# Joints between layer stages of a decoder kernel: tiles in pairs, norm factors in ScalarE's copies, one strip's split in halves

## What is computed

```
def _rmsnorm(x, g):
    xf = x.astype(jnp.float32)
    y = xf * lax.rsqrt(jnp.mean(xf * xf, axis=-1, keepdims=True) + NORM_EPS)
    return (y * g.astype(jnp.float32)).astype(x.dtype)
...
        xp = xp + _rmsnorm(mp, gn[1])
        xs = xs + _rmsnorm(ms, gn[1])
        xp = xp + _rmsnorm(_mlp(_rmsnorm(xp, gn[2]), w_ff1[layer], w_ff2[layer]), gn[3])
        xs = xs + _rmsnorm(_mlp(_rmsnorm(xs, gn[2]), w_ff1[layer], w_ff2[layer]), gn[3])
```

## Time and profile before

| | |
|---|---|
| time, median of 3 runs (lowest, highest) | 1041.13 us (1038.32, 1041.52) |
| the profiled execution's own time | 1040.35 us |
| its span | 1038.5 us |
| PE busy (matmul) | 979.0 us, 94% |
| VectorE busy | 604.4 us, 58% |
| ScalarE busy | 434.8 us, 42% |
| DMA, mean | 199 GB/s |
| mean granted TensorE clock | 0.981 of full |

### The profile page before, as it was taken

One profiled execution on the slowest core, in us unless ns is written; L12 is line 12 of the kernel. 1 busy time (PEld: TensorE's weight loads), 2 busy tenths in 40 slices (PEclk: granted clock), 3 DMA queues, 4 the chain that ended last, 5 costly groups with the idle time before them and its releaser, 6 DMA issues. The chain is left out here.

```text
span 1038.5 us, 17317 instructions
## 1 busy us (share of the span) xinstructions
PE 979.0 (94%) x7348; PEld 893.3 (86%) x7348; DVE 604.4 (58%) x767; ACT 434.8 (42%) x549; POOL 35.4 (3%) x72
## 2 busy tenths in 40 slices
PE   6999999998979999999789999999999799999994
PEld 5888998654979999999787878778799799999993
DVE  6756644547487554334775767586573775543443
ACT  5222233567455444333532443526343554543330
POOL 0310000000000000000001000000100000000000
PEclk9999999999989999999899999999999899999997
DMA  9887859636525444544544948685755244444411
GB/s 357 307 287 260 275 166 359 225 109 227 200 90 184 164 168 172 172 170 165 196 168 152 328 170 308 238 286 187 277 208 186 95 167 167 174 171 171 163 40 45
DMA packets 50444, 206.60 MB, mean 199 GB/s; under 512 B 3536, under 2 KB 3920, under 8 KB 34768
## 3 DMA queue, kind: packets, MB, share of 16 engines
q1 hardware_dynamic: 44640, 181.40, 50.0%
q0 software_dynamic: 5744, 24.33, 6.0%
HBM read 181.39 MB, written 24.33 MB: 198 GB/s over the span
## 5 line engine op out<-in xcount | busy, mean ns | idle before, releaser
L563 PE MATMUL banks<-hH,wH 128*128 128x288 f32 x1248 | 378.7, 303 | 29.8 <-DVE hL L1522 26.4
L1153 ACT ACTIVATE wH<-raw 128x2048 fp32r<-128x2048 f32 x116 | 222.2, 1916 | 376.8 <-PE banks L565 374.5
L1513 DVE TENSOR_TENSOR wL<-raw,wH 128x2048 fp32r<-128x2048 f32 x116 | 265.8, 2291 | 195.9 <-ACT wH L1153 195.7
L564 PE MATMUL banks<-hL,wH 128*128 128x288 f32 x1248 | 371.4, 298 | 0.0
L565 PE MATMUL banks<-hH,wL 128*128 128x288 f32 x1248 | 371.4, 298 | 0.0
L563 PEld LDWEIGHTS banks<-hH,wH 128*128 128x128 f32 x1248 | 239.5, 192 | 47.4 <-issue 40.1
L564 PEld LDWEIGHTS banks<-hL,wH 128*128 128x128 f32 x1248 | 238.3, 191 | 0.4
L565 PEld LDWEIGHTS banks<-hH,wL 128*128 128x128 f32 x1248 | 237.9, 191 | 0.0
L564 PE MATMUL banks<-aL,wH 128*128 128x288 f32 x512 | 151.0, 295 | 0.0
L565 PE MATMUL banks<-aH,wL 128*128 128x288 f32 x512 | 150.9, 295 | 0.0
L563 PE MATMUL banks<-aH,wH 128*128 128x288 f32 x512 | 150.2, 293 | 0.0
(11 more groups left out here) (265 smaller groups left out, 1012.9 us busy)
## 6 DMA issues: line engine op xcount, KB each, us to landing
raw<-wst SPq DMA_DIRECT2D x120, 1024.0 KB, 4.9
cache_sb<-kcache SPq DMA_DIRECT2D x14, 1024.0 KB, 6.1
sslot<-state SPq DMA_DIRECT2D x11, 1024.0 KB, 7.3
sstate_out<-sslot POOLq DMA_DIRECT2D x11, 1024.0 KB, 8.5
raw<-vcache SPq DMA_DIRECT2D x6, 1024.0 KB, 9.6
w_area<-vcache SPq DMA_DIRECT2D x6, 1024.0 KB, 13.0
raw<-state SPq DMA_DIRECT2D x5, 1024.0 KB, 8.2
sstate_out<-raw POOLq DMA_DIRECT2D x5, 1024.0 KB, 5.5
```

What stands on the lines that cost most here:

```text
L563: nc.tensor.matmul(out[:, m, :], wH[:, u % 2, c], hi[:, k, :], start=first, stop=False)
L564: nc.tensor.matmul(out[:, m, :], wH[:, u % 2, c], lo[:, k, :], start=False, stop=False)
L1153: nc.scalar.activation(wH[:, at % SPL, :], raw[:, raw_slot(at), :], ACT.Copy).then_inc(h_round, 1)
L1513: nc.vector.tensor_tensor(wL[:, at % SPL, :], raw[:, raw_slot(at), :], wH[:, at % SPL, :].bitcast(F32), ALU.subtract).then_inc(l_split, 1)
```

## The change

- **Gain.** `copy_y` multiplies by the post-norm gain while ScalarE copies y out of PSUM, one tile at a time. `residual` then needs only `y * rs_post` and the addition, both in place without `tmp`.
- **Groups.** `residual` runs over `X_GROUPS`: tiles 0 and 1 alone, then three pairs; at the end of the kernel over four pairs. The hL of a group stands behind the *next* group's multiplication. ScalarE's `pre_norm` follows the same groups, with one square for a pair.
- **Second strip.** Its split leaves the middle of the tiles and stands behind them, in two halves (`low_split`, `l_split`); PE's wL matmuls of that strip run tile by tile and wait for the halves in turn.
- **Third strip.** Its first half's split stands ahead of the three sums of squares; PE takes `mean_square` behind the fifth tile, not the second.
- **Retention.** `qpad` is cleared after p = 2, and strip 5 is split after p = 3.
- **x_out** is issued and waited for by SP, not POOL.

Nothing is put into PE's pause at a joint.

```diff
+X_GROUPS = ((0, 1), (1, 1), (2, 2), (4, 2), (6, 2))
+X_LAST = ((0, 2), (2, 2), (4, 2), (6, 2))
...
             strips(S_RETOUT + N_RETOUT, N_STRIPS)
+            for k, n in X_LAST:
+                sp.wait_ge(x_done, 3 * KT + k + n)
+                sp.dma_start(x_out[:, k:k + n, :], x[:, k:k + n, :]).then_inc(fin, 16)
+            sp.wait_ge(fin, 16 * len(X_LAST))
...
-            for k in range(0, KT, 2):
-                pool.wait_ge(x_done, 3 * KT + k + 2)
-                pool.dma_start(x_out[:, k:k + 2, :], x[:, k:k + 2, :]).then_inc(fin, 16)
-            pool.wait_ge(fin, 16 * KT // 2)
...
-                pe.wait_ge(l_split, s + 2)
-                for m in range(2):
-                    for k in range(KT):
+                pe.wait_ge(low_split, b)
+                for k in range(KT):
+                    if k == KT // 2:
+                        pe.wait_ge(l_split, s + 2)
+                    for m in range(2):
...
-                    if k == 1:
+                    if k == KT // 2:
                         mean_square(mean_d, sumsq[:, :], x_sum, 3 * b)
...
-                for k in range(KT):
-                    act.wait_ge(x_done, KT * (b - 1) + k + 1)
-                    round_x(k, layer, norm)
-                    nc.scalar.activation(y[:, k, :], x[:, k, :], ACT.Square).then_inc(xsq2, 1)
+                for k, n in X_GROUPS:
+                    act.wait_ge(x_done, KT * (b - 1) + k + n)
+                    for i in range(k, k + n):
+                        round_x(i, layer, norm)
+                    nc.scalar.activation(y[:, k:k + n, :], x[:, k:k + n, :], ACT.Square).then_inc(xsq2, n)
...
+            def copy_y(e, k, of):
+
+                return nc.scalar.activation(y[:, k, :], of, ACT.Copy, scale=gain(*POST_NORM[e], k))
+
...
-                nc.scalar.activation(y[:, 2 * j:2 * j + 2, :], out, ACT.Copy).then_inc(y_copied, 1)
+                copy_y(e, 2 * j, out[:, 0, :])
+                copy_y(e, 2 * j + 1, out[:, 1, :]).then_inc(y_copied, 1)
...
-                    dve.wait_ge(xsq2, KT * b)
-                    nc.vector.tensor_tensor(y[:, 0:4, :], y[:, 0:4, :], y[:, 4:8, :], ALU.add).then_inc(x_sum, 1)
                     dve.wait_ge(half_round, b + 1)
                     c = slice(0, HALF_STRIP)
                     nc.vector.tensor_tensor(wL[:, s % 2, c], raw[:, raw_slot(s + 2), c], wH[:, s % 2, c].bitcast(F32),
                                             ALU.subtract).then_inc(half_split, 1)
+                    dve.wait_ge(xsq2, KT * b)
+                    nc.vector.tensor_tensor(y[:, 0:4, :], y[:, 0:4, :], y[:, 4:8, :], ALU.add).then_inc(x_sum, 1)
...
-                for k in range(KT + 2):
-                    if k < KT:
-                        if k >= 2:
-                            dve.wait_ge(x_done, KT * e + k - 1)
-                        nc.vector.scalar_tensor_tensor(out=tmp[:, k % 2, :], in0=y[:, k, :], scalar=gain(layer, norm, k),
-                                                       in1=rs_post[:, :], op0=ALU.mult, op1=ALU.mult).then_inc(t_done, 1)
-                    if 1 <= k <= KT:
-                        dve.wait_ge(t_done, KT * e + k)
-                        nc.vector.tensor_tensor(x[:, k - 1, :], x[:, k - 1, :], tmp[:, (k - 1) % 2, :],
-                                                ALU.add).then_inc(x_done, 1)
-                    if k >= 2 and b is not None:
-                        split_x(b, k - 2, nlayer, nnorm)
-                    if k == 4 and s is not None:
-                        split_strip(s + SPL, s + SPL)
+                groups = X_LAST if b is None else X_GROUPS
+                behind = ()
+                for k, n in groups:
+                    c = slice(k, k + n)
+                    rs = rs_post[:, :].unsqueeze(1).broadcast_to([P, n, T])
+                    nc.vector.tensor_tensor(y[:, c, :], y[:, c, :], rs, ALU.mult).then_inc(t_done, n)
+                    for i in behind:
+                        split_x(b, i, nlayer, nnorm)
+                    dve.wait_ge(t_done, KT * e + k + n)
+                    nc.vector.tensor_tensor(x[:, c, :], x[:, c, :], y[:, c, :], ALU.add).then_inc(x_done, n)
+                    behind = range(k, k + n) if b is not None else ()
+                for i in behind:
+                    split_x(b, i, nlayer, nnorm)
+                if b is None:
+                    return
+
+                at = (s + SPL) % SPL
+                dve.wait_ge(h_round, s + SPL + 1)
+                for c, done in ((slice(0, HALF_STRIP), low_split), (slice(HALF_STRIP, KT * SC), l_split)):
+                    nc.vector.tensor_tensor(wL[:, at, c], raw[:, raw_slot(s + SPL), c], wH[:, at, c].bitcast(F32),
+                                            ALU.subtract).then_inc(done, 1)
...
-                if p == 3:
-                    nc.vector.memset(qpad[:, :, :], 0.0).then_inc(r_dec, 1)
...
                 if p == 2:
-                    split_strip(s + 3, s + 3)
+                    nc.vector.memset(qpad[:, :, :], 0.0).then_inc(r_dec, 1)
+                if p == 3:
+                    split_strip(s + 2, s + 2)
```

16 lines of the change are left out of this document (9 added, 7 removed).

## The result

The changed kernel takes 1033.28 us (median of 4 runs, 1032.43 to 1033.70), beside 1040.73 us for the kernel before in the same series (4 runs, 1038.32 to 1041.52): a ratio of 0.9929, 95% interval 0.9915 to 0.9944. It is faster by about 7.4 us. The forecast was 1035.1 us in a range of 1032.3 to 1038.3.

A forecast was written before the change was run, and what follows sets the result against it. PE, busy 94% of the span, was taken as the bound, so only its waits and half clock mattered. The terms summed to -5.63 us, giving 1034.7 or 1035.5 by starting point; forecast 1035.1 us, range 1032.3 to 1038.3.

The forecast's parts named there:

- Part 1: Start of the three joints: the first hL comes earlier and PE moves with it, -0.57 us each.
- Part 2: Third strip in joints 1 and 3: sums ahead of the second half's split make PE wait, +0.43 us each.
- Part 3: Head 0 of retention: value tile sooner, -1.85 us, and no half clock behind the shorter pause, -1.71 us.
- Part 4: Kernel's end: DVE's stretch -1.25 us, SP's earlier issue -0.27, its landing +0.3; -1.22 us in all.
- rival 1: Clock takes part back: half clock's end stays put behind the joints, +0.9 us, 1036.0, or 1037.7 with retention's; chance 0.17.
- rival 2: Head 0 in retention keeps its gap as another wait replaces the value tile's: 1038.7 us; chance 0.09.
- rival 3: At the joints the groups don't start PE earlier: 3 x 0.57 us back, 1036.8 us; chance 0.07.
- rival 4: At the end x_out's last pair lands slowly on SP's queue, 13.9 us: slower, 1046.3 us; chance 0.05.

The follow-up runs named there:

- the mixed cases: Changed kernel with x_out issued by POOL and waited for by SP, 1033.80 us; or issued by SP and waited for by POOL, 1034.89 us.

## Why the prediction was right, and which terms were off

The forecast's sign held, and its size within the range (-5.63 us against -7.3 in the profiled executions), but not because every term did. By its own steps:

| step | forecast | measured |
|---|---|---|
| Part 1, pause of a joint | -0.57 each | -0.59 each (5.37 to 4.78) |
| Part 2, third strip | +0.43 in joints 1 and 3 | +0.49 and +0.53 |
| Part 3, head 0's wait with the stall | -1.85 | -2.18 + 0.46 = -1.72 |
| Part 3, clock behind it | -1.71 | -1.71 (no stretch at half clock) |
| Part 4, DVE's stretch | -1.25 | 7.21 to 6.22, -0.99 |
| Part 4, behind the last addition | -0.27 + 0.3 = +0.03 | 5.68 to 2.55, -3.13 |
| half clock behind the joints | not in the sum (rival 1: +0.9) | +1.07 |
| the old wait for the fourth tile, joints 1 and 2 | not in the sum | -0.60 |
| ahead of joint 1 | not in the sum | +0.60 |

The measured terms, with the pause three times, add up to -7.2 us, the span's own difference. That the time fell within the range is in part luck: errors of both signs met. Without the +0.60 and the +1.07 of the clock it would have been some 1.7 us lower, below the range's 1032.3.

**Parts 1 to 3 were right**, in size and in mechanism. In Part 1 the first hL came 1.55 us behind the first product, where 1.58 was reckoned. For Part 2, from the second strip's first wL product to the fourth strip's first product it was 834.95 - 825.37 = 9.58 us in joint 3, and before 838.09 - 829.04 = 9.05: 0.53 us; in joint 1 it was 0.49, in joint 2 0.46. Part 3 was confirmed from both sides, by putting it back (+3.45 us) and by making it alone (-5). Part 1 was never undone by itself: its 0.59 us are read from the pauses, and what of them reaches the time is the question of rival 1. ScalarE's single copies, put at nothing, cost next to nothing: measured from the last product ahead of it, a joint's mean starts no later in joints 1 and 2, and 0.16 us later in joint 3.

**Part 4 had its mis-sized term**: what lies behind DVE's last addition. The prediction followed the transfer to its landing and took the rest as equal on both engines. The row "5.68 us from the last addition to the end of the span" could have been read from the earlier trace rows and the span: 0.30 to POOL's issue and 2.4 for the landing leave 3.0 us that nothing in the sum explained; 2.6 of them are the DRAIN at the end of POOL's list, a row of the trace before. With SP the same reckoning leaves 0.4 us (0.03 and 2.1 of 2.55). That part was worth three times the rest of Part 4. The landing itself went the other way than the row I relied on: 2.1 us on SP's queue against 2.4 on POOL's, -0.3 in place of +0.3.

The Trainium skill, "DMA: Bandwidth & Descriptors", section "Latency and other measured facts", puts SP's first byte some 0.4 us ahead of POOL's; no row here shows a first byte, but the landings agree with the order, 2.1 us on SP's queue and 2.4 on POOL's. The prediction had weighed this against a load's 2.7 us and stayed with the load; that row was of another transfer, and the page was nearer.

DVE's stretch was 0.26 us longer than reckoned, since an addition follows its product by 0.11 us at 128x576 (1022.53 + 0.76 to 1023.40), not by the 0.04 of the smaller dependent sums; four such gaps are 0.28.

**A term that the sum lacked: the old wait for the fourth tile.** In joint 2 of the kernel before, DVE's hL of the fourth tile, and PE's first product of that tile:

```profile
508.90 0.52 DVE L1522 SCALAR_TENSOR_TENSOR hL<-x,col,hH 128x288 fp32r<-128x288 f32 x1
```

```profile
509.48 0.40 PE L563 MATMUL banks<-hH,wH 128*128 128x288 f32 x1
```

PE starts 0.06 us behind the hL, which stood behind the whole split of the second strip, where the product ahead of it (509.09) would have let it start at 509.22. With a slower first product behind the hold this cost 0.36 us, and 0.24 in joint 1. There the half clock had lasted 3.3 and 3.6 us; in joint 3, with 4.8, PE came later and lost nothing. The split's new place takes these 0.60 us away. It is the same wait as the 1.57 us that the filled pause brought out in the kernel before.

**Rival 1 stays open, and this profile went its way.** The half clock behind the joints was 5.69 + 4.96 + 3.16 = 13.8 us after and 3.62 + 3.26 + 4.79 = 11.7 before, half of the difference being the +1.07. Two profiles do not show the cause. The kernel before with only the output's engine changed has joints of the old kind and even longer stretches:

```profile
292.08:297.26 5.18, 5.18 (x22) 0.50 0.02 3
504.46:508.90 4.44, 4.43 (x18) 0.50 1.07 422
816.99:822.89 5.90, 5.90 (x25) 0.50 0.08 12
```

15.5 us in all, and the kernel before with only retention changed has 3.71 + 3.47 + 2.78 = 10.0. But over all profiles with an empty pause, the six with pauses of 4.78 us have 13.8 to 16 us at half clock behind the joints, 14.6 in the mean, and the three with 5.37 have 10.0 to 15.5, 12.4 in the mean. Half of these 2.2 us is 1.1, near the rival's 0.9; with three profiles on one side this is not told from chance. So how much of the 1.77 us of shorter pauses reaches the time is not shown. The Trainium skill, "TensorE: Matmul & The Clock Gate", section "What's actually happening", says that the chip's watch on PE runs freely; the trace agrees so far as equal pauses of 4.78 us were followed by 3.16 to 5.69 us at half clock.

The shift of 0.60 us ahead of joint 1 is chance: in attention, which the change leaves as it was, the clock was low for 2.98 us in the profile before and 5.87 after, which took 1.28 us, against 0.69 us by which PE was ahead until then. With POOL for both it was not low there at all.

**Rivals 2, 3 and 4 did not happen.** Head 0's wait went (rival 2), each joint's first hL came 0.6 us earlier (rival 3), and SP's landing was 2.1 us, not 13.9 (rival 4). What should have shown the steps right came out nearly as written: pauses of 4.78 us, head 0's wait at 1.07 with no slow clock behind it, DVE's end at 6.2 us, and the new wait in the third strip. That wait is 0.26 us by the row, where 0.43 was reckoned; by the starts PE was held 0.42. The last product ahead of it began at 830.61, the next could have begun 0.13 us later, at 830.74, and began at 831.16. The product behind it follows 0.24 us later in place of 0.13, which makes the 0.53 us.

What stays open: whether the shorter pauses bring longer half clock with them (rival 1), and what POOL's DRAIN does in its time.

## What to carry to other kernels

Read the time behind the last instruction of a compute engine as a term of its own (span's end less that instruction's end), compare it with the landing of the last transfer, look for what the engines still run behind it (here POOL's DRAIN of 2.3 to 3.3 us), and try which engine issues and waits for it. A pause of a matmul engine that cannot be closed may still be filled: but the fill pays only where the data then come as fast as the engine at full clock asks, so first move out whatever stands in the middle of the feeding list. And when two things hold the same instruction (late sums, a late mean), undoing one only brings out the other: read which releaser the row names after the edit. A wait row of PE can miss a short hold; compare the starts of equal products.

## What the runs showed of the hardware

- The end of a program with 288 KB as the last transfer came 2.5 us behind the last DVE instruction with SP issuing and waiting (2.55, 2.50 in two kernels), and 5.7 us behind it with POOL (5.68, 5.66); 4.24 and 4.75 in the mixed cases. POOL's DRAIN at the end of its list took 2.28 to 3.29 us, SP's 0.12 at most.
- A wait of 3.25 us on PE was followed by about 3.4 us at half clock in each of the four profiles that had it; waits of 1.07 and 0.19 us at the same place were followed by none. Behind pauses of 4.78 us the half clock lasted between 3.16 and 5.69 us in one execution. With the pause filled up to the last 0.31 us it did not occur.
- At full clock products of 288 columns start 0.13 us apart; behind a hold by a semaphore the next one follows the first by 0.24 us (831.16 to 831.40).
- On DVE a 128x576 addition that needs the product just ahead starts 0.11 us behind its end; one that does not starts 0.08 us before it. Over four pairs that was 0.77 us.
